# Stick-breaking attention of the later 512 tokens, computed between the expert rows by tanh, scan and product

## The chip, the cores and the metric

One core of one Trainium2 chip runs the whole program. The metric is the device time in microseconds (us) of one execution. The engines named below are PE (TensorE, matrix products and transposes), DVE (VectorE), ACT (ScalarE), POOL (GpSimd) and SP (SyncE, which here only issues DMAs).

## The reference, cut to what matters

One layer for 1024 tokens of 1024 features, float32: a mixer (gated linear attention beside stick-breaking attention, 8 heads of 64), an attention over 256 memory tokens, and PEER, in which each token gathers 128 expert rows (8 heads of 16) out of 16384.

```
z = q.k / 8 over all earlier tokens;  log_1m = log_sigmoid(-z) where s < t, else 0
A[t, s] = sigmoid(z_ts) * prod_{s<j<t} (1 - sigmoid(z_tj));  o_t = sum_s A[t, s] v_s        # 8 heads
h += [gla | o] @ w_out;  h += MemCrossAttn(rmsnorm(h))
h += sum over 128 experts e(t) of gate * gelu(u[e] . rmsnorm(h)) * v[e]                      # row of u|v: 8 KB
out = rmsnorm(h)
```

## The kernel before, in words

The tokens are split in halves of 512 (four blocks of 128 each). The mixer's projections are made for all 1024 tokens. `stick_phase` (from line 1569) then computes stick-breaking attention of both halves. Its unit of work is a tile: 128 keys on the partitions, up to 512 queries of one half on the columns, two heads at a time. `work` lists 48 pairs of tiles: per pair of heads four key blocks for the first half, eight for the second. Per tile PE makes z, ACT takes Abs, Exp, Ln (lines 1657 to 1659), DVE adds the positive part (line 1685), PE turns that into sums over later keys with a triangular product and a product with a running `carry` (lines 1721, 1725), ACT exponentiates (line 1650) and PE multiplies with the values (line 1751). GpSimd masks the diagonal tiles (line 1621). Six buffers lie between the engines.

After it come, for the first half alone, the output projection (`mixer_out_phase`), which also loads the residual x of all tokens into `co.H` (four loads of 1 MB), memory attention, and the first half's expert scores. Then `expert_phase` (from line 2207) runs through 1024 steps R, one for each of 128 experts of each of 8 token blocks:

- GpSimd gathers 128 rows of 8 KB (line 2014) into one of seven ring slots. It may reuse a slot once PE has read it (`row_used`).
- DVE takes the dot product of the row's first half with the token (line 2524), and runs one piece of the selection of the experts two groups ahead (`choice.select`, 16 pieces for each 16 rows).
- ACT takes Gelu (line 2626), multiplies by the gate (line 2628), scales the row's second half (line 2635), and once in 16 rows takes an Exp for the gate (line 1914).
- PE adds the row to an accumulator by eight transposes (line 2754).

Beside the rows, each engine has a function `later(R)` that runs the second half's remaining work at steps written in the table `Later`: the output projection (MIX, 64 matmul units, one a step), a norm, the memory query, the attention over memory (UNIT = 10 steps for each of 8 units), its output, a norm, and the second half's scores (KEYS), which must be there when the second half's rows begin at R = 512. The weights of these products come by SP through four slots `w_raw`. The order on each engine is the program's order, so an instruction that waits holds back all that its engine does later.

Shared state: `scratch`, `hb`, `own_acc`, `qt`, `w_raw` are buffers of the expert phase; `side[0..3]` are four PSUM banks for the work beside the rows.

Of the kernel before, what the change touches and what calls it, by code (L numbers as in the profile page):

```python
# [8 lines left out]
F32 = mybir.dt.float32  # L9
# [1559 lines left out]
def stick_phase(co, feat, tok, spare, mix_t, mix_b, negtri, negone):  # L1569
# [10 lines left out]
    NH = SEQ // HALF  # L1580
    QB = HALF // P
    S = 6
    PAIRS = SB_HEADS // 2

    rounds = [(-1, 0, 1), (0, 1, 7), (0, 1, 6), (-1, 0, 0), (0, 1, 5), (0, 1, 4), (0, 0, 3), (0, 1, 3), (0, 0, 2),
              (0, 1, 2), (0, 1, 1), (0, 1, 0)]
    work = [(pr + d, th, j, max(0, j - QB * th) * P) for pr in range(PAIRS + 1) for d, th, j in rounds
            if 0 <= pr + d < PAIRS and (pr < PAIRS or d)]  # L1590
    begun = [min(i for i, w in enumerate(work) if w[0] == pr) for pr in range(PAIRS)]
    M = len(work)
    N = 2 * M
    tile = lambda m: work[m // 2]
    diag = [tile(m)[2] >= QB * tile(m)[1] for m in range(N)]
    same = lambda n, m: n % 2 == m % 2 and tile(n)[1] == tile(m)[1]
    before = [max([n for n in range(m) if same(n, m)], default=None) for m in range(N)]
    ended = [w[:2] for w in work if w[2] == 0]

    adds = [0 if tile(m)[2] == 0 else (1 if not diag[m] else (2 if tile(m)[3] + P < HALF else 1)) for m in range(N)]  # L1600

    def upto(flags, n):

        return sum(flags[:n + 1])

    with ExitStack() as cx:
# [3 lines left out]
        carry = co.sb("stick_carry", [P, 2, NH, 2, HALF], ctx=cx)  # L1610
        pz = [cx.enter_context(nc.psum_tensor(f"stick_pz{j}", [P, HALF], F32)) for j in range(S)]
        po = [cx.enter_context(nc.psum_tensor(f"stick_po{j}", [P, HALF], F32)) for j in range(NH)]
        block = cx.enter_context(nc.Block())

        @block.gpsimd
        def _(pool):
            co.clear_stale(pool)

            def strict(ap, c0, done):

                pool.affine_select(out=ap[:, c0:c0 + P], in_=ap[:, c0:c0 + P], compare_op=ALU.is_gt, fill=0.0,  # L1621
                                   base=0, pattern=[[1, P]], channel_multiplier=-1).then_inc(done, 1)

            for i in range(M + 2):
                for n in (2 * i - 4, 2 * i - 3):
                    if n >= 0 and diag[n]:
                        pool.wait_ge(a_ready, n + 1)
                        strict(aw[:, n % S, :], tile(n)[3], a_masked)
                for m in (2 * i, 2 * i + 1):
                    if i < M and diag[m]:  # L1630
                        pool.wait_ge(sp_ready, m + 1)
                        strict(sps[:, m % S, :], tile(m)[3], sp_masked)

        @block.scalar
        def _(act):
# [3 lines left out]
            def queries(pr):  # L1639
                nc.scalar.activation(feat[:, pr, :], feat[:, pr, :], ACT.Copy, scale=SB_DH ** -0.5).then_inc(q_ready, 1)  # L1640

            queries(0)
            for i in range(M + 2):
                for n in (2 * i - 4, 2 * i - 3):
                    if n >= 0:
                        c0, s = tile(n)[3], n % S
# [4 lines left out]
                for m in (2 * i, 2 * i + 1):  # L1651
                    if m < N:
                        c0, s = tile(m)[3], m % S
# [6 lines left out]
                if i in (2, 3, 4):  # L1660
                    queries(i - 1)

        @block.vector
        def _(dve):

            for i in range(M + 5):
                n = 2 * (i - 4) + 1
                if 0 <= n < N and tile(n)[2] == 0:
                    pr, th, _, _ = tile(n)
                    dve.wait_ge(pv_done, n + 1)  # L1670
                    if th:
                        nc.vector.tensor_copy(mix_b[:, GLA_HEADS + pr, :], po[th][:, :]).then_inc(o_free, 1)
                    else:
                        hi, lo = (x[:, GLA_HEADS + pr, 0:HALF] for x in mix_t)
                        nc.vector.tensor_copy(hi, po[th][:, :]).then_inc(hi_ready, 1)
                        dve.wait_ge(hi_ready, pr + 1)
                        low(nc, lo, po[th][:, :], hi).then_inc(o_free, 1)
                two = (2 * i, 2 * i + 1) if i < M else ()
                for m in two:
                    c0, s = tile(m)[3], m % S  # L1680
                    if m >= S:
                        dve.wait_ge(carry_ready, upto(adds, m - S))
# [4 lines left out]
                for m in two:  # L1687
                    _, th, j, c0 = tile(m)
                    h, s = m % 2, m % S
                    if j > 0:  # L1690

                        k = QB * th + QB - 1 - j
                        new, old = carry[:, h, th, k % 2, :], carry[:, h, th, (k + 1) % 2, :]
                        if before[m] is not None:
                            dve.wait_ge(r_full, before[m] + 1)
                        c1 = c0 + P if diag[m] else c0
                        if diag[m]:
                            dve.wait_ge(sp_masked, upto(diag, m))
                        else:
                            dve.wait_ge(sp_ready, m + 1)  # L1700
                        if c1 < HALF:
                            dve.wait_ge(carry_ready, upto(adds, before[m]))
                            nc.vector.tensor_tensor(new[:, c1:], old[:, c1:], sps[:, s, c1:], ALU.add).then_inc(carry_ready, 1)
                        if diag[m]:
                            nc.vector.tensor_copy(new[:, c0:c1], sps[:, s, c0:c1]).then_inc(carry_ready, 1)

        @block.tensor
        def _(pe):
            for i in range(M + 3):
                if 0 <= i - 2 < M:  # L1710
                    _, th, j, c0 = work[i - 2]
                    for h in range(2):
                        n = 2 * (i - 2) + h
                        s = n % S
                        if diag[n]:
                            pe.wait_ge(sp_masked, upto(diag, n))
                        else:
                            pe.wait_ge(sp_ready, n + 1)
                        k = QB * th + QB - 1 - j
                        c1 = c0 + P if diag[n] else c0  # L1720
                        last = nc.tensor.matmul(pz[s][:, c0:], negtri[:, :], sps[:, s, c0:], start=False,  # L1721
                                                stop=(c1 == HALF), skip_group_check=True)
                        if c1 < HALF:
                            pe.wait_ge(carry_ready, upto(adds, before[n]))
                            last = nc.tensor.matmul(pz[s][:, c1:], negone[:, :], carry[:, h, th, (k + 1) % 2, c1:],
                                                    start=False, stop=True, skip_group_check=True)
                        last.then_inc(r_full, 1)
                if i < M:
                    pr, th, j, c0 = work[i]
# [4 lines left out]
                    for h in range(2):  # L1734
                        rows = slice(h * SB_DH, (h + 1) * SB_DH)
                        nc.tensor.matmul(pz[(2 * i + h) % S][:, c0:], feat[rows, F_KS - F_QS + pr, j * P:(j + 1) * P],
                                         feat[rows, pr, th * HALF + c0:(th + 1) * HALF], start=True, stop=False,
                                         skip_group_check=True).then_inc(z_full, 1)
                if 0 <= i - 3 < M:
                    pr, th, j, c0 = work[i - 3]  # L1740
                    n = 2 * (i - 3)
                    first = j == QB * th + QB - 1
                    if first and pr:
                        pe.wait_ge(o_free, ended.index((pr - 1, th)) + 1)
                    if diag[n]:
                        pe.wait_ge(a_masked, upto(diag, n + 1))
                    else:
                        pe.wait_ge(a_ready, n + 2)
                    for h in range(2):
                        rows = slice(h * SB_DH, (h + 1) * SB_DH)  # L1750
                        nc.tensor.matmul(po[th][rows, c0:], v[:, j, pr * P + h * SB_DH:pr * P + (h + 1) * SB_DH],
# [406 lines left out]
class Later:  # L2158
# [5 lines left out]
    NORM = 35  # L2164
    MIX = 2
    QNORM = MIX + 2 * KT * 4 + 3
    QUERY = QNORM + NORM
    ATTEND = QUERY + 2 * KT * 4 + 4
    UNIT = 10
    OUT = ATTEND + NB * UNIT + 12  # L2170
    FNORM = OUT + 2 * KT * 4 + 3
# [4 lines left out]
    def __init__(self):  # L2176
        begin = [self.MIX + 4 * p for p in range(2 * KT)] + [self.QUERY + 4 * p for p in range(2 * KT)]
        begin += [self.OUT + 4 * p for p in range(2 * KT)] + [self.KEYS + 4 * p for p in range(4 * PH)]
        self.fetch = {begin[i - self.SLOTS] + 4: i for i in range(self.SLOTS, self.N)}
        self.unit = {begin[i] + j: (i, j) for i in range(self.N) for j in range(4)}  # L2180
        self.add = {at + 32 * c + 31 + b: (2 * e + c, b) for e, at in enumerate((self.MIX, self.OUT))
                    for c in range(2) for b in range(4)}
        self.kept = {self.QUERY + 8 * m + 10: m for m in range(KT)}
        units = [(self.ATTEND + self.UNIT * u, u) for u in range(NB)]
        self.scores = {at + 2 * j: (u, j) for at, u in units for j in range(2)}
        self.maxima = {at + 5: u for at, u in units}
        self.exps = {at + 6: u for at, u in units}
        self.probs = {at + 8: u for at, u in units}
        self.turn = {at + 10: u for at, u in units}
        self.turned = {at + 12: u for at, u in units}  # L2190
        self.values = {at + 15 + 2 * j: (u, j) for at, u in units for j in range(2)}
        self.attended = {at + 20: u for at, u in units}
        norms = [(e, at) for e, at in enumerate((self.QNORM, self.FNORM))]
        self.square = {at + 1 + b: (e, b) for e, at in norms for b in range(4)}
        self.var = {at + 8: e for e, at in norms}
        self.guess = {at + 9: e for e, at in norms}
        self.refine = {at + 12 + j: (e, j) for e, at in norms for j in range(4)}
        self.scale = {at + 17 + 4 * b: (e, b) for e, at in norms for b in range(4)}
        self.across = {at + 19 + 4 * b: (e, b) for e, at in norms for b in range(4)}
        self.gain = {at + 22 + 4 * b: (e, b) for e, at in norms for b in range(4)}  # L2200
# [6 lines left out]
def expert_phase(co, choice, ring, scores, rstd, uv, gf, g_final, out, k_t, v_m, z_b, mix_b, w_out, w_mq, w_mo, w_pq,  # L2207
                 sub_keys, q_gain, gain):
# [21 lines left out]
    def pe_rows(R):  # L2230
# [19 lines left out]
        sem(n) for n in ("m_scored", "m_max", "m_probs", "m_normed", "m_turned", "m_turned_sb", "m_full", "o_kept"))  # L2250
    q_b = o_b = mix_b
    with ExitStack() as cx:
# [25 lines left out]
        m_stat = sb("m_stat", [P, 2, 4, 2])  # L2278
        m_ps = [side_ps[:, j, :].rearrange("p (h m) -> p h m", h=2) for j in range(2)]
        m_pt = [side_ps[:, 2 + j, :].rearrange("p (f t) -> p f t", t=P) for j in range(2)]  # L2280
        m_po = [side_ps[:, j, :].rearrange("p (f t) -> p f t", t=P) for j in range(2)]
        block = cx.enter_context(nc.Block())

# [29 lines left out]
        def _(sp):  # L2313
# [16 lines left out]

            for i in range(at.SLOTS):
                fetch(i)
# [617 lines left out]
```

## Time and profile before

| | us |
|---|---|
| median of 3 runs | 3633.78 (3633.17 to 3634.96) |
| the profiled execution | 3628.59, its span 3626.4 |
| PE, DVE, ACT, POOL busy | 2664.3, 2289.4, 2346.3, 1256.3 |

The profile is of one execution. Busy times of PE overlap with each other and are modelled at their ends. The stick phase begins after 384 us and ends at 593 us of the span; the expert phase begins at 967 us and ends with the span.

### The profile page before, as it was taken

How to read it: one execution, taken by the hardware profiler on the slowest of the kernel's cores; microseconds unless marked ns; L12 is line 12 of the kernel's file. 1: busy time of each engine (PE TensorE's matmuls, PEld its weight loads, DVE VectorE, ACT ScalarE, POOL GpSimd, SP SyncE). 2: the span in 40 equal slices, each digit the busy share in tenths (PEclk: the TensorE clock that was granted, in tenths of full speed). 3: DMA queues.
4: the chain of work that ended last, by engine and by line, in shares of the span. 5: the costliest groups of instructions: out<-in, count | busy, mean ns of one | idle time of the engine just before them, and what ended most of it. 6: DMA issues, size and time to landing. Idle time of an engine off the chain costs nothing.

```text
span 3626.4 us, 41556 instructions
## 1 busy us (share of the span) xinstructions
PE 2664.3 (73%) x13816; PEld 2003.4 (55%) x13816; DVE 2289.4 (63%) x5474; ACT 2346.3 (65%) x4227; POOL 1256.3 (35%) x1176
## 2 busy tenths in 40 slices
PE   7999998888877676667767777666666666666666
PEld 6777444777745544654455544555555554555554
DVE  4554444544566776777677666766676676667665
ACT  3221785423377777887687767777777777777775
POOL 0000110000234443444344334444444454444443
PEclk9999999999998899889979999767666667666666
DMA  2001002321599999999999999999999999999998
GB/s 111 18 19 47 1 1 102 119 82 58 220 420 420 419 420 415 406 415 420 420 414 420 419 418 410 410 416 418 417 412 416 417 410 416 417 416 410 419 415 339
DMA packets 177654, 1156.70 MB, mean 319 GB/s; under 512 B 19984, under 2 KB 22048, under 8 KB 46240
## 3 DMA queue, kind: packets, MB, share of 16 engines
q0 software_dynamic: 147456, 1073.81, 71.7%
q1 hardware_dynamic: 29984, 80.26, 6.1%
q8 instruction: 107, 1.75, 0.2%
q14 instruction: 107, 0.88, 0.1%
HBM read 1149.80 MB, written 4.19 MB: 318 GB/s over the span
## 4 chain that ended last, share of the span: by engine, by line
DMA 40%; ACT 14%; PE 8%; DVE 6%; issue 5%; POOL 1%; POOLq 0%; DVEq 0%; ACTq 0%
DMA early_rows<-in_uv,choice_index 24%; DMA rows<-in_uv,choice_index 16%; PE expert_acc L2754 7%; ACT early_rows L2635 4%; DVE early_rows L2524 3%; ACT rows L2635 2%; ACT L2626 2%; ACT L1914 2%; DVE rows L2524 2%; ACT expert_wt L2628 2%; ACT expert_wt L2626 1%; ACT choice_best L1914 1%; POOL rows L2014 0%; POOL early_rows L2014 0%; PE expert_acc L2741 0%
## 5 line engine op out<-in xcount | busy, mean ns | idle before, releaser
L2754 PE MATMUL expert_acc<-ident,early_rows 128*128 128x128 f32 x4648 | 826.6, 338 | 492.7 <-ACT early_rows L2635 492.0
L2754 PEld LDWEIGHTS expert_acc<-ident,early_rows 128*128 128x128 f32 x4648 | 680.7, 175 | 731.9 <-ACT early_rows L2635 704.2
L2524 DVE CUSTOM_DVE_ANT_0 early_rows<-early_rows,expert_xn 128x1024 f32<-128x1024 f32 x586 | 718.9, 1227 | 461.0 <-DMA early_rows<-in_uv,choice_index 459.3
L2014 POOL DMA_INDIRECT early_rows<-in_uv,choice_index x586 | 692.0, 1181 | 888.8 <-PE expert_acc L2754 742.4
L2754 PE MATMUL expert_acc<-ident,rows 128*128 128x128 f32 x3480 | 622.1, 340 | 369.4 <-ACT rows L2635 369.2
L2754 PEld LDWEIGHTS expert_acc<-ident,rows 128*128 128x128 f32 x3480 | 513.8, 177 | 545.3 <-ACT rows L2635 522.5
L2524 DVE CUSTOM_DVE_ANT_0 rows<-rows,expert_xn 128x1024 f32<-128x1024 f32 x438 | 537.1, 1226 | 339.6 <-DMA rows<-in_uv,choice_index 337.9
L2014 POOL DMA_INDIRECT rows<-in_uv,choice_index x438 | 514.6, 1175 | 644.2 <-PE expert_acc L2754 554.4
L2635 ACT ACTIVATE early_rows<-early_rows,expert_wt 128x1024 f32<-128x1024 f32 x581 | 667.3, 1149 | 18.9
L2626 ACT ACTIVATE expert_wt<-expert_dot 128x1 f32<-128x1 f32 x1024 | 204.9, 200 | 624.7 <-DVE expert_dot L2524 623.1
L2635 ACT ACTIVATE rows<-rows,expert_wt 128x1024 f32<-128x1024 f32 x435 | 499.6, 1149 | 14.2
L2628 ACT ACTIVATE expert_wt<-expert_wt,choice_gate 128x1 f32<-128x1 f32 x1024 | 301.5, 294 | 33.2
L2673 PE MATMUL expert_side<-z_b,expert_w_raw 128*128 128x512 f32 x256 | 135.3, 612 | 0.0
L2658 PE MATMUL expert_side<-expert_w_raw,mix_b 128*128 128x512 f32 x256 | 134.4, 607 | 0.0
L1685 DVE SCALAR_TENSOR_TENSOR heads<-stick_pz,stick_t 128x512 f32<-128x512 f32 (+3 forms) x96 | 53.5, 557 | 102.4 <-ACT stick_t L1659 102.2
L1621 POOL TENSOR_SCALAR_AFFINE_SELECT heads<-heads 128x128 f32<-128x128 f32 x64 | 20.7, 323 | 258.4 <-DVE heads L1685 258.2
L2626 ACT ACT_TABLE_LOAD x80 | 102.6, 1283 | 4.0 <-DVE expert_dot L2524 2.6
L2046 POOL IOTA choice_iota<- 128x16 f32 x1 | 0.1, 145 | 270.9 <-issue 270.9
L1721 PE MATMUL stick_pz<-heads,negtri 128*128 128x512 f32 (+3 forms) x192 | 83.5, 523 | 1.8 <-POOL heads L1621 1.2
L2524 DVE DVE_READ_ACCUMULATOR2_ANT expert_dot<- 128x1 f32 x1024 | 83.9, 82 | 0.0
L1914 ACT ACT_TABLE_LOAD x62 | 79.5, 1283 | 1.1
L1361 ACT ACTIVATE heads<-gla_po 128x256 f32<-128x256 f32 x16 | 5.3, 381 | 95.1 <-PE gla_po L1415 95.1
(369 smaller groups left out, 3956.2 us busy)
## 6 DMA issues: line engine op xcount, KB each, us to landing
early_rows<-in_uv,choice_index POOLq DMA_INDIRECT x586, 12.4
H<-in_x SPq DMA_DIRECT2D x8, 1024.0 KB, 10.6
pq_w_raw<-in_w_pq SPq DMA_DIRECT2D x16, 512.0 KB, 3.5
expert_w_raw<-in_w_pq SPq DMA_DIRECT2D x32, 256.0 KB, 9.0
rows<-in_uv,choice_index POOLq DMA_INDIRECT x438, 12.3
stick_w_raw<-in_w_feat SPq DMA_DIRECT2D x8, 512.0 KB, 3.5
tok_w_raw<-in_w_tok SPq DMA_DIRECT2D x8, 512.0 KB, 3.7
out_w_raw<-in_w_out SPq DMA_DIRECT2D x8, 512.0 KB, 4.2
```

The lines of the kernel that those rows point to most:

```text
L1621: pool.affine_select(out=ap[:, c0:c0 + P], in_=ap[:, c0:c0 + P], compare_op=ALU.is_gt, fill=0.0, base=0, pattern=[[1, P]], channel_multipl ...
L1685: nc.vector.scalar_tensor_tensor(sps[:, s, c0:], pz[s][:, c0:], 0.0, t[:, s, c0:], ALU.max, ALU.add).then_inc(sp_ready, 1)
L1721: last = nc.tensor.matmul(pz[s][:, c0:], negtri[:, :], sps[:, s, c0:], start=False, stop=(c1 == HALF), skip_group_check=True)
L1914: self.nc.scalar.activation(self.best[:, q, :], self.best[:, q, :], ACT.Exp, bias=self.small[:, 0, q:q + 1], accum_out=self.small[:, 1, q: ...
L2014: pool.indirect_dma_start(out=self.rows[R % self.ROWS], out_offset=None, in_=uv, in_offset=bass.IndirectOffsetOnAxis(ap=index, axis=0), bo ...
L2524: nc.vector.tensor_tensor_reduce(rows[R % ROWS][:, 0:D], rows[R % ROWS][:, 0:D], xn[:, :], 1.0, 0.0, ALU.mult, ALU.add, dot[:, h % 2, r:r ...
L2626: link(nc.scalar.activation(wt[:, s, 0, r:r + 1], dot[:, s, r:r + 1], ACT.Gelu))
L2628: weight = nc.scalar.activation(wt[:, s, 1, r:r + 1], wt[:, s, 0, r:r + 1], ACT.Copy, scale=gate[:, q, r:r + 1])
L2635: nc.scalar.activation(v, v, ACT.Copy, scale=wt[:, s, 1, r:r + 1]).then_inc(row_scaled, 1)
L2658: last = nc.tensor.matmul(side[j], mix_b[:, k, j * P:(j + 1) * P], w_raw[:, slot, :], start=k == 0, stop=k == KT - 1)
L2673: last = nc.tensor.matmul(side[n % 2], w_raw[:, slot, j * P:(j + 1) * P], x, start=k == 0, stop=k == KT - 1)
L2754: last_mm = nc.tensor.matmul(acc[:, k * P:(k + 1) * P], rows[R % ROWS][:, D + k * P:D + (k + 1) * P], co.ident[:, :], start=(r == 0 and k ...
```

## The change

`stick_phase` keeps the first half alone: 16 pairs of tiles, all on the diagonal, two pairs of heads interleaved (`LANES = 2`). On SP it gets DMAs that park data in HBM: the values v (2 MB), the second half's queries (1 MB), and `w`, the difference of each token's value and the value before it (2 MB), for which v is read back shifted by one token. DVE makes the four differences. `vcol` holds v at the block borders, by four loads of single elements.

The second half's attention is done in `expert_phase` in 32 turns (head by query block), one every 5 rows from R = 2. With 1 - sigmoid(z) = (1 - tanh(z/2))/2, a scan from the last key to the first gives the running product, and the product of that with w gives the output less the query's own value. Per turn: PE makes z with the queries on the partitions (640 to 1024 keys), ACT takes Tanh one step later, GpSimd halves it (`m * -0.5 + 0.5`) between two gathers, DVE scans it, PE transposes it, ACT copies it, PE multiplies with w, DVE adds `vcol`. `mix_b` gets the result. The x of the second half (2 loads of 1 MB) is loaded after the last turn instead of in `mixer_out_phase`. The table `Later` starts its old work at R = 168 instead of 2, in a closer order: three units in two steps, 26 steps for a norm instead of 35, UNIT = 7, and KEYS at R = 417 instead of 366.

```diff
-    rounds = [(-1, 0, 1), (0, 1, 7), ...]
-    work = [(pr + d, th, j, max(0, j - QB * th) * P) for pr in range(PAIRS + 1) for d, th, j in rounds
-            if 0 <= pr + d < PAIRS and (pr < PAIRS or d)]
+    work = [(pr + lane, j, j * P) for pr in range(0, PAIRS, LANES) for j in range(QB - 1, -1, -1) for lane in range(LANES)]
...
+        @block.sync
+        def _(sp):
+            sp.dma_start(park_v[1:SEQ + 1, :].rearrange("(b p) c -> p b c", p=P), v).then_inc(v_parked, 16)
+            sp.wait_ge(zeroed, 1)
+            sp.dma_start(park_v[0:1, :], zero[:, :]).then_inc(v_parked, 16)
+            sp.dma_start(park_q.rearrange("r p t -> p r t"), feat[:, 0:PAIRS, HALF:SEQ]).then_inc(q_parked, 16)
+            sp.wait_ge(v_parked, 32)
+            sp.dma_start(v_last[:, :, :], park_v[0:SEQ, :].rearrange("(b p) c -> p b c", p=P)).then_inc(shifted, 16)
+            for b in range(QB):
+                sp.dma_start(vcol[:, b, :], ...).then_inc(columns, 16)
+            sp.wait_ge(w_ready, NB // 2)
+            for pr in range(PAIRS):
+                sp.dma_start(park_w[pr]..., v_last[:, :, pr * P:(pr + 1) * P]).then_inc(w_parked, 16)
+            sp.wait_ge(q_parked, 16)
+            sp.wait_ge(columns, 16 * QB)
+            sp.wait_ge(w_parked, 16 * PAIRS)
...
+                if i in DIFF:
+                    b = 2 * DIFF[i]
+                    dve.wait_ge(shifted, 16)
+                    nc.vector.tensor_tensor(v_last[:, b:b + 2, :], v_last[:, b:b + 2, :], v[:, b:b + 2, :],
+                                            ALU.subtract).then_inc(w_ready, 1)
...
+    STICK, TURNS, STEP = 2, 4 * SB_HEADS, 5
+    MIX = STICK + STEP * (TURNS - 1) + 11
+        turns = [(self.STICK + self.STEP * u, u) for u in range(self.TURNS)]
+        self.z, self.tanh, self.halve, self.scan, self.flip, self.flipped, self.weigh, self.stick = (
+            {at + after: u for at, u in turns} for after in (0, 1, 2, 3, 6, 7, 8, 10))
...
                     ring.gather(pool, R, index[:, q, r:r + 1], uv)
+                    if R - ROWS + 1 in at.halve:
+                        u = at.halve[R - ROWS + 1]
+                        pool.wait_ge(tanh_ready, u + 1)
+                        pool.tensor_scalar(m, m, -0.5, 0.5, ALU.mult, ALU.add).then_inc(halved, 1)
...
+                if R in at.scan:                                                  # DVE
+                    dve.wait_ge(halved, u + 1)
+                    nc.vector.tensor_tensor_scan(m, m, m, 1.0, ALU.mult, ALU.min).then_inc(scanned, 1)
+                if R in at.stick:
+                    dve.wait_ge(o_full, u + 1)
+                    nc.vector.tensor_scalar(mix_b[...], side[2][feats, 0:P], vcol[...], None, ALU.add).then_inc(o_taken, 1)
...
+                if R in at.tanh:                                                  # ACT
+                    act.wait_ge(z_full, u + 1)
+                    nc.scalar.activation(probs[u % 2][:, 0:ended], z_ps[:, 0:ended], ACT.Tanh,
+                                         scale=0.5 * SB_DH ** -0.5).then_inc(tanh_ready, 1)
+                if R in at.flipped:
+                    act.wait_ge(p_turned, u + 1)
+                    nc.scalar.activation(probs_t[:, 0:ended], flip_ps[:, 0:ended], ACT.Copy).then_inc(p_kept, 1)
...
+                if R in at.z:                                                     # PE
+                    nc.tensor.matmul(z_ps[:, 0:HALF], q, co.H[feats, HB + pr, 0:HALF], start=True, stop=True)
+                    nc.tensor.matmul(z_ps[:, HALF:ended], q, co.H[feats, HB + pr, HALF:ended], ...)
+                    nc.tensor.matmul(z_ps[:, ended - P:ended], co.ident[:, :], above[:, :], ...).then_inc(z_full, 1)
+                if R in at.flip:
+                    pe.wait_ge(scanned, u + 1)
+                    for j in range(ended // P):
+                        last = nc.tensor.transpose(flip_ps[:, cols], probs[u % 2][:, cols], co.ident[:, :])
+                if R in at.weigh:
+                    for j in range(ended // P):
+                        last = nc.tensor.matmul(side[2][feats, 0:P], pair_w[pr][:, j, feats], probs_t[:, j * P:(j + 1) * P], ...)
```

## Rows read from the trace of the kernel before

**Rows 1.** Stages: stretch, length, busy PE PEld DVE ACT POOL, PEclk, DMA share, GB/s.
```profile
384.00:593.00 209.00, 202.75 (x736) 85.92 (x736) 101.39 (x228) 182.36 (x390) 39.64 (x128) 0.98 0.00 1
...
967.00:3627.00 2660.00, 1786.23 (x9248) 1359.81 (x9248) 1833.62 (x4634) 1949.40 (x3518) 1201.97 (x1020) 0.79 1.00 413
...
1000.00:1178.00 178.00, 129.65 (x645) 83.19 (x644) 119.38 (x302) 129.42 (x234) 73.32 (x67) 0.90 1.01 420
...
1413.00:1650.00 237.00, 152.79 (x968) 134.96 (x968) 178.44 (x453) 200.39 (x365) 108.98 (x93) 0.83 1.00 410
```

**Rows 2.** Groups by form, stick phase, ACT: busy us, mean ns, idle before.
```profile
L1657 ACT ACTIVATE stick_t<-stick_pz 128x512 f32<-128x512 f32 x48 | 28.3, 589 | 3.0 <-PE stick_pz L1736 3.0
L1658 ACT ACTIVATE stick_t<-stick_t 128x512 f32<-128x512 f32 x48 | 30.2, 630 | 1.5
L1650 ACT ACTIVATE tok<-stick_pz 128x512 f32<-128x512 f32 x48 | 26.8, 588 | 9.0 <-PE stick_pz L1725 9.0
L1658 ACT ACTIVATE stick_t<-stick_t 128x128 f32<-128x128 f32 x16 | 5.0, 310 | 0.5
```

**Rows 3.** Instructions in order of time, the stick phase's ends: start us, us.
```profile
383.84 1.28 ACT L1637 ACT_TABLE_LOAD   x1 [0.47 <-ACTq L1534]
...
387.07 0.28 ACT L1657 ACTIVATE stick_t<-stick_pz 128x128 f32<-128x128 f32 x1 [0.88 <-PE stick_pz L1736]
...
589.07 0.60 ACT L1650 ACTIVATE tok<-stick_pz 128x512 f32<-128x512 f32 x1 [0.91 <-PE stick_pz L1725]
...
592.93 1.28 ACT L823 ACT_TABLE_LOAD   x1 [3.26 <-PEq L1606]
```

**Rows 4.** The chain that ended last, one row's way through the engines: start us, us.
```profile
1018.91 1.23 DVE rows L2524
1020.17 0.21 ACT expert_wt L2626
1020.41 0.30 ACT expert_wt L2628
1020.74 1.16 ACT rows L2635
1021.94 1.11 PE expert_acc L2754 x8
1023.10 0.73 issue
```

**Rows 5.** Instructions in order of time: a gather's issue, and DVE with rows already landed.
```profile
1023.82 0.99 POOL L2014 DMA_INDIRECT rows<-in_uv,choice_index  x1 [1.52 <-PE expert_acc L2754]
...
971.66 1.20 DVE L2524 CUSTOM_DVE_ANT_0 early_rows<-early_rows,expert_xn 128x1024 f32<-128x1024 f32 x1
...
973.32 1.21 DVE L2524 CUSTOM_DVE_ANT_0 early_rows<-early_rows,expert_xn 128x1024 f32<-128x1024 f32 x1
```

**Rows 6.** Lines L1174 (ns min/median/max) and, by form, POOL: nearest to scan and halving.
```profile
L1174 DVE TENSOR_TENSOR_SCAN decay<-decay_keep,decay_gate x2: 2291/2291/2291, 115.7 to 126.7; 128x1024 f32<-128x1024 f32 x2
...
L1253 POOL COPY gla_vb<-heads 128x512 f32<-128x512 f32 x2 | 1.6, 802 | 0.0
L1086 POOL MEMSET decay_keep<- 128x1024 f32 x1 | 1.0, 953 | 72.5 <-issue 72.5
```

**Rows 7.** DMAs: size, us from issue to landing (of L2014: min/median/max).
```profile
DMA to landing us min/median/max: 5.8/12.4/15.1
...
H<-in_x SPq DMA_DIRECT2D x8, 1024.0 KB, 10.6
out<-expert_hb SPq DMA_DIRECT2D x8, 512.0 KB, 9.8
```

**Rows 8.** The page's groups: table loads ahead of Gelu and Exp; the products beside the rows.
```profile
L2673 PE MATMUL expert_side<-z_b,expert_w_raw 128*128 128x512 f32 x256 | 135.3, 612 | 0.0
...
L2626 ACT ACT_TABLE_LOAD x80 | 102.6, 1283 | 4.0 <-DVE expert_dot L2524 2.6
...
L1914 ACT ACT_TABLE_LOAD x62 | 79.5, 1283 | 1.1
```

More of the change, by code:

```diff
@@ L1579, in stick_phase @@
     q_ready, act_done, hi_ready = sem("q_ready"), sem("act_done"), sem("hi_ready")
-    NH = SEQ // HALF
+    zeroed, v_parked, q_parked, shifted, columns, w_ready, w_parked = (
+        sem(n) for n in ("zeroed", "v_parked", "q_parked", "shifted", "columns", "w_ready", "w_parked"))
+    park_v, park_q, park_w = park
     QB = HALF // P
@@ L1594, in stick_phase, with upto @@
     tile = lambda m: work[m // 2]
-    diag = [tile(m)[2] >= QB * tile(m)[1] for m in range(N)]
-    same = lambda n, m: n % 2 == m % 2 and tile(n)[1] == tile(m)[1]
+    same = lambda n, m: n % 2 == m % 2 and tile(n)[0] % LANES == tile(m)[0] % LANES
     before = [max([n for n in range(m) if same(n, m)], default=None) for m in range(N)]
[L1598 to L1604, printed above, removed]
+    adds = [0 if tile(m)[1] == 0 else (2 if tile(m)[2] + P < HALF else 1) for m in range(N)]
+    DIFF = {6 + 2 * d: d for d in range(NB // 2)}
+    def upto(n):
+        return sum(adds[:n + 1])
     with ExitStack() as cx:
@@ L1639, in queries @@
             def queries(pr):
[L1640 removed]
+                nc.scalar.activation(feat[:, pr, 0:HALF], feat[:, pr, 0:HALF], ACT.Copy, scale=SB_DH ** -0.5).then_inc(q_ready, 1)
             queries(0)
+            queries(1)
             for i in range(M + 2):
@@ L2176, in __init__ @@
     def __init__(self):
[L2177 to L2182, printed above, removed]
@@ L2192, in __init__ @@
-        self.attended = {at + 20: u for at, u in units}
+        third = [2 * x // 3 for x in range(8 * KT)]
+        rows = [self.MIX + x for x in third] + [self.QUERY + x for x in third] + [self.OUT + x for x in third]
+        rows += [self.KEYS + x for x in range(16 * PH)]
+        self.fetch = {rows[4 * (i - self.SLOTS) + 3] + 1: i for i in range(self.SLOTS, self.N)}
+        self.unit, self.add = {}, {}
+        for x, R in enumerate(rows):
+            self.unit.setdefault(R, []).append((x // 4, x % 4))
@@ new lines, in __init__ @@
+        units = [(self.ATTEND + self.UNIT * u, u) for u in range(NB)]
+        self.scores = {at + j: (u, j) for at, u in units for j in range(2)}
+        self.maxima = {at + 2: u for at, u in units}
+        self.exps = {at + 3: u for at, u in units}
+        self.probs = {at + 5: u for at, u in units}
+        self.turn = {at + 6: u for at, u in units}
+        self.turned = {at + 8: u for at, u in units}
+        self.values = {at + 9 + j: (u, j) for at, u in units for j in range(2)}
+        self.attended = {at + 12: u for at, u in units}
@@ L2346, in _ @@
             co.clear_stale(pool)
+            pool.memset(above[:, :], -1.0e30).then_inc(mask_ready, 1)
+            pool.wait_ge(mask_ready, 1)
+            pool.affine_select(out=above[:, :], in_=above[:, :], compare_op=ALU.is_ge, fill=0.0, base=0,
+                               pattern=[[1, P]], channel_multiplier=-1).then_inc(mask_ready, 1)
             def group(g, q):
@@ L2422, in later @@
             def later(R):
+                if R in at.scan:
+                    u = at.scan[R]
+                    _, _, _, ended = turn(u)
+                    dve.wait_ge(halved, u + 1)
+                    m = probs[u % 2][:, ended - 1::-1]
+                    nc.vector.tensor_tensor_scan(m, m, m, 1.0, ALU.mult, ALU.min).then_inc(scanned, 1)
+                if R in at.stick:
+                    u = at.stick[R]
+                    pr, feats, b, _ = turn(u)
+                    dve.wait_ge(o_full, u + 1)
+                    nc.vector.tensor_scalar(mix_b[feats, GLA_HEADS + pr, b * P:(b + 1) * P], side[2][feats, 0:P],
+                                            vcol[feats, b, pr:pr + 1], None, ALU.add).then_inc(o_taken, 1)
                 if R in at.maxima:
```

243 lines of the change are left out of this document (157 added, 86 removed).

## The prediction

> **What bounds the kernel now.** I read the stages first, by busy time in stretches, then the groups of the stick phase, then the chain that ended last, then the single operations that come nearest to the new ones.
>
> The stages [rows 1] show two different machines. In the stick phase (384 to 593 us) ACT is busy for 182.36 of 209 us while the DMA engines move 1 GB/s: ACT's four operations per tile set the pace, and the DMA engines are free. From 967 us to the end it is the reverse. The DMA share is 1.00 over 2660 us at 413 GB/s, with no compute engine above 73% (ACT). A gather is 128 rows of 8 KB, 1.049 MB, so at the 420 GB/s of the calm stretch it takes 2.50 us; 2660 us over 1024 steps are 2.60 us a step, the rest being weights and stores. A step that computes more costs nothing there as long as each engine, and each loop of waits through several engines, stays under some 2.5 us per step.
>
> The change takes ACT-bound time away where the DMA engines idle, and puts the work, and 5 MB of traffic, where the DMA engines are full. Three things decide: what the short stick phase costs, what the traffic costs, and whether a turn of five steps still fits in 5 x 2.50 = 12.5 us.
>
> **Stick phase, what goes.** The old one runs from the table load at 383.84 to the next phase's at 592.93 us, 209.1 us [rows 3]. The new one has 32 tiles (16 pairs), eight of each width 512, 384, 256, 128. ACT needs for a 512-wide tile 0.589 + 2 x 0.630 + 0.588 = 2.44 us; the Abs, Exp and Ln of a 128-wide one are about 0.3 each by the 0.310 of its Exp, with the second Exp 1.2 in all [rows 2]. Cost grows evenly with width, so the mean over the four widths is (2.44 + 1.2) / 2 = 1.82 and 32 tiles take 58 us. The same count for before (48 wide tiles at 2.44, 16 of each other width at 2.0, 1.6 and 1.2) gives 194 us, against 589.67 - 387.07 = 202.6 us measured [rows 3], so 1.04 times the count: 61 us. Around it stay 3.2 us at the start and 3.3 us at the end [rows 3], and about 2 us of query scaling and of DVE's four differences. Sum 70 us, a gain of 139 us.
>
> The new DMAs lie beside it. Parking v (2 MB), reading it back shifted behind the parked queries (1 MB), and writing w (2 MB) are a chain through SP. A 1 MB load landed in 10.6 us and a store of 512 KB in 9.8 us, both partly in company of other traffic [rows 7]; by these v is parked and read back some 25 us into the phase, near the sixth pair, where DVE first waits for it. The last difference comes at pair 12 of 16, about 50 us in, and the 2 MB of w need another 5 (420 GB/s) to 39 us (four stores one after another at 9.8); I take 18, so the phase ends at 384 + 71. With the worst it ends 20 us later. The four loads of single elements lie between; no row shows such a load, and I bound them by 0 and by the store's 9.8 us each, hidden by the compute up to about 20 us together. Net stick gain: 138 us, 115 to 141.
>
> **Traffic in the expert phase.** Queries and w come back (1 + 2 MB) and x moves in (2 MB): 5.2 MB, at 413 GB/s 12.7 us if the DMA engines stay full [rows 1]. Where the turns themselves are slower than the DMA engines, the 3 MB read in the turns cost nothing, and 5 us remain for x. Taking x's 2 MB out of the mixer's output phase saves nothing: that phase starts with weights, and 1 MB of memory tokens still comes with it.
>
> **The turn as a loop.** This is where I expect the loss. GpSimd halves turn u only behind the gather of step h + 6 (h is the turn's third step), and that gather waits until PE has read row h - 1. DVE at step h + 1 waits for the halving, with all later dot products behind it, and row h + 4, which releases the next turn's halving, is one of them. So one lap is five steps long:
> - from the start of the dot product of row h - 1 through Gelu, gate, scaling, PE's eight transposes and 0.73 us of issue to the gather: 1023.82 - 1018.91 = 4.91 us [rows 4, 5];
> - the gather's issue 0.99 us [rows 5];
> - the halving of 640 to 1024 columns, 832 in the mean. No row has it. A fill of 1024 took 0.953 us, so 0.8 is the low end; a copy of 512 took 0.802, so 1.3 is a high end by width [rows 6]. I take 1.0, nearer to the fill, plus 0.35 for the two handovers;
> - the scan: 2.291 us for 1024 columns [rows 6], by width 1.9 us in the mean;
> - the rest of step h + 1 on DVE (selection, 0.35 us), two intervals of dot products with rows already landed, 1.66 us each [rows 5], and the addition of `vcol`, 0.25.
>
> Sum 4.91 + 0.99 + 1.35 + 1.9 + 0.35 + 3.32 + 0.25 = 13.1 us, above 12.5. Two things lengthen it at times: PE's z matmuls (a 128x512 product shows 612 ns [rows 8]) stand one row ahead of row h - 1, worth 0.3 us, and the Exp of the gate with its two table loads of 1283 ns [rows 8] falls into the dependent part of about 6 of 32 laps, 0.3 us in the mean. I take 13.7. Between gathers that land early or late (5.8 to 15.1 us [rows 7]) the ring evens out bursts, but not a lap that is always longer. 32 turns then take 438 us instead of 400: 38 us lost.
>
> By load alone the engines fit: ACT 5 x 1.89 (129.42 of 178 us at 2.60 a step [rows 1]) + two operations of some 0.9 us = 11.3 us; DVE 5 x 1.74 + 2.15 = 10.9; on PE a turn's three z products, its transposes and its products with w (about 3 us, an estimate by the 612 ns of a 512-column product [rows 8]) stand where five 512-column units stood before.
>
> The SBUF page of the Trainium skill (SBUF — State Buffer, Who interferes with whom) says that a VectorE instruction with two SBUF inputs and a GpSimd one that reads SBUF block each other for a whole instruction. In the loop DVE is idle when the halving runs, so by that rule too the lap stays 13.7; where DVE is not waiting, the rule would put up to 1.2 us of a dot product before the halving. No row before shows such a pair.
>
> **What is packed closer.** The old work now runs at 1.5 units per step, and the memory attention at 7 steps a unit. ACT was busy for 200.39 of 237 us there, 22.0 us per unit of 10 steps; less three steps of 1.89 it is 16.3 of 17.5 us [rows 1]. DVE asks for the maxima one step behind the score matmuls instead of three, and waits about 1 us per unit. It fits, barely; I take 6 us for both, 0 to 15. KEYS still ends 25 steps ahead of its use. The first turn's queries come with the first gathers: 2 us.
>
> **Sum.** Against the profiled execution, 3628.6: -138 (stick) + 38 (turns) + 5 (x) + 6 (closer packing) + 2 (start) = -87, 3541.6 us. The runs' median is 5.2 us above that execution, so 3547 us.
>
> **Rivals.**
> 1. All hidden, 3511 us. The lap stays under 12.5 us because narrow blocks (640 columns: scan 1.4, halving 0.8) make up for wide ones. Then only traffic counts: 3633.8 - 138 + 12.7 + 2. For it: the DMA share of 1.00 with all engines under 85% [rows 1]. Against: the lap's rows already add up to 13.1. Chance 0.25, 3500 to 3525.
> 2. A longer turn, 3600 us. Tanh may need its own table beside Gelu's: two loads of 1.283 us per turn bring ACT to 13.9 us plus the catching up; or halving and dot products exclude each other for 1 to 2 us. Either makes the lap about 15.4: 3547 + 32 x 1.7 = 3601. No run before shows tanh.
> 3. The stick phase's DMAs end last: single elements and w take 20 to 30 us more than the compute, 3570 us. For it: the four w stores hang on the last difference. Chance 0.05.
> 4. The other side, slower. GpSimd has never done arithmetic between gathers here. If a switch between the two kinds costs it time, that time is in the lap in full. It decides from 13.7 + 87/32 = 16.4 us a lap, so at 2.7 us more per turn than I count; at 4 us more the time is 3547 + 128 = 3675. For it: gathers issue in 0.99 us but one that follows closely takes up to 2 us; against: a fill or copy needs under 1 us. Chance 0.07.
>
> The forecast has the rest, 0.43, with its own range of 3525 to 3575. The range over the cases runs from 3506, inside rival 1, to 3602, the centre of rival 2. A change under 0.2% (7 us) could not be told from none. Slower by more: rival 4 from its deciding point, 0.06; within: 0.02; faster: 0.92.
>
> **What would show it.** Stick phase: from its first table load to the next phase's about 71 us; if SP's stores end after ACT by over 5 us, rival 3. Turns: step time between R = 2 and 162 about 2.74 us with a DMA share clearly under 1.00 and 385 GB/s; DVE's scan waiting on POOL by 1.5 to 3 us each time shows the loop, a share of 1.00 shows rival 1. A table load in front of each Tanh shows rival 2. A halving over 2 us, or gathers behind it over 2 us, shows 4. After R = 545 nothing changes: 2.60 us a step. The prediction is wrong if the lap's longest part is another, such as ACT, or if the compressed norm or attention steps lose more than 15 us.

## The result and the profile after

The changed kernel takes 3603.38 us (3596.47 to 3604.11, 4 runs) against 3633.48 for the one before; ratio 0.9915, interval 0.9898 to 0.9932. It is faster by 30 us, 0.85% and clear of the noise, where 87 us were forecast. The profiled execution took 3596.47 us; before it was 3628.59, so the traces differ by 32.

The phases, from the trace after. Instructions in order of time (start, duration), ACT and SP; they answer to [rows 3]:

```profile
384.37 1.28 ACT L1659 ACT_TABLE_LOAD   x1 [0.47 <-ACTq L1534]
...
450.62 1.28 ACT L823 ACT_TABLE_LOAD   x1 [3.41 <-PEq L1606]
...
432.64 4.27 SPq L1630 DMA_DIRECT2D park_w<-stick_v_last  x4
...
484.37 43.71 SPq L318 DMA_DIRECT2D mk_w_raw<-in_w_mk  x8
```

The stick phase is 66.3 us long (209.1 before). Its last stores are issued before 437 us; such a store landed 5.4 us after its issue in the median, so they hide behind the compute, which ends at 447 us. Stages, with the columns of [rows 1]:

```profile
817.00:1328.00 511.00, 364.67 (x2110) 283.81 (x2111) 347.88 (x809) 348.96 (x614) 268.23 (x200) 0.86 0.91 345
...
1640.00:1830.00 190.00, 125.77 (x782) 110.03 (x781) 130.32 (x340) 155.11 (x284) 79.01 (x69) 0.84 0.96 385
...
2200.00:3590.00 1390.00, 917.29 (x4526) 734.85 (x4524) 945.12 (x2370) 999.04 (x1803) 652.37 (x535) 0.71 1.00 411
```

In the 32 turns (817 to 1328 us) the DMA engines move 345 GB/s instead of the 420 of the calm stretch before, and no compute engine is above 72% of its time. Some loop of waits sets the pace. Who waits, 820 to 1320 us (total, times, longest):

```profile
DVE expert_w_raw L2503 <- POOL expert_w_raw L2433: 137.4, 32, 9.8
...
ACT expert_w_raw L2658 <- PE expert_side L2798: 52.5, 25, 4.8
...
DVE mix_b L2508 <- PE expert_side L2817: 15.9, 12, 3.4
...
DVE rows L2611 <- DMA rows<-in_uv,choice_index: 4.5, 2, 3.4
```

Before, DVE's main wait was for rows to land. Now rows have landed and DVE waits at each of the 32 scans for GpSimd's halving, 4.3 us in the mean. The new operations themselves are short (ns min/median/max):

```profile
L2433 POOL TENSOR_SCALAR expert_w_raw<-expert_w_raw x32: 735/900/1061, 833.8 to 1315.9; 128x640 f32<-128x640 f32 x8, 128x768 f32<-128x768 f32 x8, 128x896 f32<-128x896 f32 x8, 128x1024 f32<-128x1024 f32 x8
...
L2503 DVE TENSOR_TENSOR_SCAN expert_w_raw<-expert_w_raw x32: 1491/1892/2293, 834.6 to 1317.0; 128x640 f32<-128x640 f32 x8, 128x768 f32<-128x768 f32 x8, 128x896 f32<-128x896 f32 x8, 128x1024 f32<-128x1024 f32 x8
```

One lap in order of time, from the dot product of row h - 1 at 1084.62 us. ACT has scaled that row at 1087.6 us, but PE first does z for the coming tanh (L2795 to L2798), then the row; only then come the gather, the halving and the scan:

```profile
1084.62 1.22 DVE L2611 CUSTOM_DVE_ANT_0 rows<-rows,expert_xn 128x1024 f32<-128x1024 f32 x1
...
1086.32 1.12 PE L2795 MATMUL expert_side<-H,expert_spare 64*128 64x512 f32 x2
...
1086.44 1.15 ACT L2739 ACTIVATE rows<-rows,expert_wt 128x1024 f32<-128x1024 f32 x1
...
1087.28 0.59 PE L2796 MATMUL expert_side<-H,expert_spare 64*128 64x256 f32 x2
...
1087.80 0.49 PE L2798 MATMUL expert_side<-expert_above,ident 128*128 128x128 f32 x2
1088.13 1.04 PE L2895 MATMUL expert_acc<-ident,rows 128*128 128x128 f32 x8
...
1089.96 0.99 POOL L2029 DMA_INDIRECT rows<-in_uv,choice_index  x1 [1.73 <-PE expert_acc L2895]
...
1090.98 0.84 POOL L2433 TENSOR_SCALAR expert_w_raw<-expert_w_raw 128x768 f32<-128x768 f32 x1
...
1091.86 1.76 DVE L2503 TENSOR_TENSOR_SCAN expert_w_raw<-expert_w_raw 128x768 f32<-128x768 f32 x1 [2.93 <-POOL expert_w_raw L2433]
```

Averaged over the turns, from the starts and ends of these instructions, a lap is 15.6 us, and 32 of them are the 499 us that steps 2 to 162 took: dot product to gather 7.0 (5.3 in the lap above), gather 1.0, halving with its handovers 1.0, scan 1.9, rest of the step 0.4, the two intervals of dot products 1.7 and 2.6.

### The profile page after: what moved, and what is told of

It reads as the page before. It is cut to its first block, busy times and chain, and to the rows that moved or that the text cites. A ratio compares the mean times of both kernels' runs of the same rounds, so it can differ in the third digit from the quotient of the medians.

```text
span 3594.8 us, 41774 instructions
## 1 busy us (share of the span) xinstructions
PE 2669.4 (74%) x14136; PEld 2061.8 (57%) x14136; DVE 2279.1 (63%) x5394; ACT 2259.8 (63%) x4033; POOL 1322.2 (37%) x1147
## 4 chain that ended last, share of the span: by engine, by line
DMA 30%; ACT 17%; PE 14%; DVE 8%; issue 6%; POOL 2%; POOLq 0%; DVEq 0%; ACTq 0%
DMA early_rows<-in_uv,choice_index 19%; DMA rows<-in_uv,choice_index 10%; PE expert_acc L2895 9%; ACT early_rows L2739 4%; DVE early_rows L2611 3%; ACT rows L2739 3%; ACT L2730 2%; ACT expert_wt L2732 2%; ACT L1929 2%; DVE rows L2611 2%; ACT expert_wt L2730 1%; PE expert_side L2764 1%; POOL early_rows L2029 1%; DVE expert_w_raw L2503 1%; PE expert_side L2795 1%
## 5 line engine op out<-in xcount | busy, mean ns | idle before, releaser
L2029 POOL DMA_INDIRECT early_rows<-in_uv,choice_index x586 | 725.9, 1239 | 939.4 <-PE expert_acc L2895 764.2
L2029 POOL DMA_INDIRECT rows<-in_uv,choice_index x438 | 536.7, 1225 | 595.6 <-PE expert_acc L2895 521.8
L2503 DVE TENSOR_TENSOR_SCAN expert_w_raw<-expert_w_raw 128x640 f32<-128x640 f32 (+3 forms) x32 | 60.5, 1891 | 137.4 <-POOL expert_w_raw L2433 137.4
L2658 ACT ACTIVATE expert_w_raw<-expert_side 128x640 f32<-128x640 f32 (+3 forms) x32 | 27.6, 862 | 53.7 <-PE expert_side L2798 52.5
L158 ACT ACTIVATE pq_w_hi<-pq_w_raw 128x1024 fp32r<-128x1024 f32 x16 | 16.9, 1056 | 69.4 <-PE keys_pq L171 67.8
```

The lines of the kernel that those rows point to most:

```text
L2029: pool.indirect_dma_start(out=self.rows[R % self.ROWS], out_offset=None, in_=uv, in_offset=bass.IndirectOffsetOnAxis(ap=index, axis=0), bo ...
L2503: nc.vector.tensor_tensor_scan(m, m, m, 1.0, ALU.mult, ALU.min).then_inc(scanned, 1)
L2658: nc.scalar.activation(probs[u % 2][:, 0:ended], z_ps[:, 0:ended], ACT.Tanh, scale=0.5 * SB_DH ** -0.5).then_inc(tanh_ready, 1)
```

## The experiments

Ratios are to the kernel before on the same chip, with 95% intervals. A ratio's worth in us is taken against 3628 us.

**Scan two steps later.**
```diff
-            {at + after: u for at, u in turns} for after in (0, 1, 2, 3, 6, 7, 8, 10))
+            {at + after: u for at, u in turns} for after in (0, 1, 2, 5, 8, 9, 10, 12))
```
The stages behind the turns start two steps later too.

> The changed kernel with the scan and all behind it two steps later in each turn (scan at step 5 of the turn instead of 3, transposes 8, copy 9, product 10, addition 12; the later stages start 2 steps later). Theory loop: a lap runs from the dot product of row h-1 over ACT, PE, the gather, the halving and the scan to the dot product of row h+4, 15.6 us in the trace of the changed kernel. With the scan two steps later two intervals of dot products (1.71 + 2.59 us) fall out of it, so it is 11.3 us and the DMA engines set the pace: steps 2 to 162 at about 2.6 us instead of 3.12, GB/s in that stretch from 345 to over 400, the time about 3603 - 80 = 3523 us (3505 to 3545). Rival load: the turns are slow because an engine or the DMA engines have more to do; then it stays at 3603 within 8. Rival GpSimd: a gather that follows arithmetic is slower by itself; then it also stays near 3603.

Measured 3588.1 us, ratio 0.9887 (0.9870 to 0.9904): 10 us won, not 80. The theory in this form fell. The waits show why (820 to 1300 us):

```profile
POOL early_rows L2029 <- PE expert_acc L2895: 99.9, 41, 7.6
DVE mix_b L2508 <- PE expert_side L2817: 99.5, 26, 10.1
```

The wait for the halving is gone (4.5 us are left of 129), and 99.5 us of waiting for PE's product with w stand in its place. Steps 2 to 162 took 484 us, 15.1 a turn. There is a second handover behind the first, over DVE, ACT and PE without GpSimd. But this edit also made it worse: a turn starts every 5 steps, so the product, now at step 10, falls into the same step as the z of the turn two later. In 30 of 32 turns PE does it right behind z; in the changed kernel in none. Two lines of this run in order of time, the end of a turn's z and the product of the turn two before:

```profile
1085.87 0.49 PE L2798 MATMUL expert_side<-expert_above,ident 128*128 128x128 f32 x2
1086.29 1.96 PE L2817 MATMUL expert_side<-expert_spare,expert_own_acc 128*64 128x128 f32 x16
```

How much of the 99.5 us comes from this meeting and how much from the handover was not separated.

**No halving at all.** GpSimd's instruction is left out, so the later half's attention is wrong; `dve.wait_ge(halved, u + 1)` becomes `dve.wait_ge(tanh_ready, u + 1)`.

> The changed kernel without GpSimd's halving; the scan waits for the tanh instead and scans it as it is, so the attention of the later half is wrong. Theory loop: GpSimd, the gather ahead of it and PE leave the lap, which is now dot product of h-1, ACT, tanh, scan, two dot products: about 1.3 + 1.7 + 1.0 + 0.9 + 1.9 + 0.4 + 4.3 = 11.5 us; DMA bound, about 3525 us (3505 to 3545), as with the later scan, although the same DVE, ACT and PE work is done. Rival load: only GpSimd's 32 x 0.9 us of work goes, and GpSimd is at 52% there, so no more than 10 us are won: 3593 or above. Rival GpSimd (arithmetic between gathers is dear): also about 3525, and so told apart by the run with the later scan alone.

Measured 3540.75 us, ratio 0.9759 (0.9743 to 0.9776): 57 us less for leaving out 29 us of work on an engine that was half idle. DVE still waited 63.7 us for the product with w, which may be why it did not reach 3525. Between these two runs it stayed open whether GpSimd's arithmetic is dear in itself.

**z one step earlier.**
```diff
-            ... for after in (0, 1, 2, 3, 6, 7, 8, 10))
+            ... for after in (-1, 1, 2, 3, 6, 7, 8, 10))
```

> The changed kernel with each turn's three z matmuls one step earlier (step -1 of the turn instead of 0), so that they no longer stand on PE right ahead of the transposes of row h-1. Theory loop: the 1.36 us between ACT's end and PE's start in the lap fall to about 0.3, the lap from 15.6 to 14.6 us: 32 x 1.0 = 32 us less, 3571 us (3560 to 3585). Rival load: PE's work is the same, so nothing changes: 3603 within 8. If PE were not in the lap at all, also 3603.

Measured 3598.96 us, ratio 0.9916 (0.9900 to 0.9933): nothing. The expectation missed. ACT's end to PE's start did fall from 1.3 to 0.6 us in the mean, but PE's end to the gather rose from 0.9 to 1.9: z now delays the row before, and with it the gather queued ahead of the one that counts. PE is in the lap for all it does in a few rows.

**The scan and the addition later.** Steps (0, 1, 2, 5, 8, 9, 10, 13).

> As the run with the later scan (scan at step 5 of a turn, transposes 8, copy 9, product with w 10), and DVE's addition of vcol at step 13 instead of 12, three steps behind the product on PE. In the run with the scan alone DVE's wait for the halving (129 us in the turns) was gone, and a wait of 99.5 us for the product with w stood in its place. Theory chains: every step that couples DVE to PE or GpSimd with two steps or less between them makes a lap of its own; with the addition three steps behind, part of the 99 us goes: 3588 - 20 = 3568 us (3545 to 3580). Rival load: what is left is work on PE at a low clock and on ACT; then 3588 within 8 and the wait shows up on another pair.

Measured 3571.59 us, ratio 0.9842 (0.9824 to 0.9861), 16 us better than with the scan alone; the wait for the product is down from 99.5 to 68.7 us. The product is still at step 10, behind a z.

**All couplings apart.**
```diff
-            ... for after in (0, 1, 2, 3, 6, 7, 8, 10))
+            ... for after in (0, 2, 3, 6, 9, 10, 11, 14))
-    MIX = STICK + STEP * (TURNS - 1) + 11
+    MIX = STICK + STEP * (TURNS - 1) + 15
```

> All couplings of a turn drawn apart: z at 0, tanh 2 (was 1), halving 3, scan 6 (three steps behind the halving instead of one), transposes 9, copy 10, product 11, addition 14. The same work on each engine as in the changed kernel. Theory chains: the waits are hidden, steps 2 to 162 take 2.60 to 2.70 us instead of 3.12, and the time is 3597 - 70 = 3527 us (3510 to 3550). Rival load (PE at half clock, ACT with its table loads, DVE): the work of a turn does not fit beside five rows whatever the order; then steps of 2.95 us and more and a time above 3570.

Measured 3527.75 us, ratio 0.9725 (0.9709 to 0.9742): 69 us better than the changed kernel with exactly its work. The stage, and two of the waits (820 to 1240 us): DVE waits for landing rows again.

```profile
817.00:1262.00 445.00, 339.79 (x2124) 268.95 (x2125) 372.80 (x822) 350.33 (x621) 267.97 (x202) 0.89 0.98 399
```
```profile
DVE early_rows L2611 <- DMA early_rows<-in_uv,choice_index: 25.9, 34, 2.3
DVE rows L2611 <- DMA rows<-in_uv,choice_index: 22.5, 24, 3.4
```

The rival by load is out: DVE is busy for 84% of this stretch and ACT for 79%, and it fits.

Against the run before this one only two things differ, apart from all steps behind z being one later: tanh stands two steps behind z instead of one, and the product no longer falls into the step of a z. Together they are worth 42 us, more than the later scan and addition (27). ACT's wait for z went with them, 52.2 us before and 3.5 here. Which of the two counts was not tested.

**The halving on DVE.** Steps as in the changed kernel; DVE does `tensor_scalar(m, m, -0.5, 0.5, mult, add)` before the scan.

> The halving done by DVE just before the scan instead of by GpSimd, steps as in the changed kernel. Theory chains: GpSimd, its gather and PE leave the lap, DVE gets 32 x 0.5 to 0.9 us more. The run without halving was at 3541, so about 3541 + 10 = 3551 us (3545 to 3575), 45 us better than with GpSimd's help. Rival: DVE is the bound, and taking work from it is what counts; then it is no better than the changed kernel, 3597 or more.

Measured 3546.66 us, ratio 0.9775 (0.9758 to 0.9791). DVE needs 486 to 692 ns for it, 19 us in all, and the kernel is 51 us faster than with GpSimd's help. All other distances are as in the changed kernel, so of the 69 us that the version with couplings apart gained, GpSimd's place in the lap was worth about 51. DVE still waits 47.1 us for the product, which shows the second handover without the meeting of product and z.

**The memory attention one step later.**
```diff
-        self.maxima = {at + 2: u for at, u in units}
+        self.maxima = {at + 3: u for at, u in units}
```
and all behind it likewise.

> The changed kernel with the memory attention's maxima, and all behind them, one step later in each unit (the maxima two steps behind the last score product instead of one); UNIT stays 7. In the changed kernel the stretch from 1640 to 1830 us moves 385 GB/s instead of about 418. Theory chains: DVE's wait for the scores is the cause; the stretch comes back to about 410 GB/s, 8 to 12 us less: 3587 us. Rival load: ACT's table loads fill the units (16.3 of 17.5 us by count); then no change, 3597 within 5.

Measured 3587.02 us, ratio 0.9883 (0.9867 to 0.9900), 12 us less than the changed kernel (the two intervals overlap slightly; the stretch shows it better). The stretch from 1640 us, against 385 GB/s above:

```profile
1640.00:1830.00 190.00, 126.99 (x815) 110.32 (x814) 140.35 (x359) 163.56 (x302) 86.34 (x72) 0.88 1.00 412
```

**x moved alone, in the kernel before.** `loads[2:4]` issued behind the first four weights of the expert phase; the add waits for them.

> The kernel before with one part of the change alone: the second half's x (2 MB) is loaded at the start of the expert phase instead of in the mixer's output phase. The changed kernel's mixer output phase was 6.6 us shorter than before (33.7 instead of 40.3 us from its first weight load to the next phase's). Theory: its two x loads less did that, so here too the phase is 6 to 7 us shorter and the expert phase is 5 us longer (2.1 MB at 418 GB/s): 3632 us, within 5 of before. Rival: something else shortened it, such as the memory tokens' place; then the phase stays at 40 us and the time is 3638.

Measured 3630.35 us, ratio 1.0003 (0.9993 to 1.0012). SP's issues show the mixer's output phase at 33.6 us (592.72 to 626.27) instead of 40.3 and DVE's dot products show the expert phase's steps 2 to 42 at 2.79 us instead of 2.65. What the one phase gains, the other gives back: the kernel's time is unchanged. The issues:

```profile
592.72 0.80 SPq L318 DMA_DIRECT2D out_w_raw<-in_w_out  x2
...
626.27 43.69 SPq L318 DMA_DIRECT2D mk_w_raw<-in_w_mk  x8
```

**Both edits together, and who halves then.**

> The turns with all couplings drawn apart (first of the two edits, 70 us) and the memory attention's maxima one step later (second, 10 us), together. Theory chains: the two waits lie in different stretches, so their gains add: 3597 - 80 = 3517 us (3508 to 3525), with the DMA engines at 400 GB/s or more from 820 us on. Rival: what one frees the other stretch gives back, 3527.

> As the run with both edits, and the halving on DVE. Theory chains: once the couplings are apart, it does not matter which engine halves as long as it has time; DVE is at 84% of its time there and gets 0.5 to 0.9 us a turn more, GpSimd is at 60%: 3517 to 3527 us, equal or a little slower than with GpSimd. Rival: GpSimd's arithmetic itself costs gathers; then this one is faster by 10 us or more.

> The changed kernel once more, beside the two above on one chip: 3597 us within 6 (ratio to before 0.9915).

Measured: 3518.31 us, ratio 0.9700 (0.9687 to 0.9713) with GpSimd halving; 3517.84, 0.9696 (0.9683 to 0.9709) with DVE halving; 3598.74, 0.9922 (0.9907 to 0.9937) for the changed kernel again. The gains add, 80 us in all, and the result is 3.0% under the kernel before. Apart, it does not matter who halves, within the 5 us that the intervals allow. That closes what the runs with the later scan and without halving left open: GpSimd's arithmetic adds nothing to the kernel's time. It does not relieve DVE either. In the stage DVE is busy for 379.74 us with GpSimd halving and for 376.70 with its own halving in them; the last section shows why. The stage with GpSimd halving:

```profile
817.00:1262.00 445.00, 346.77 (x2149) 274.89 (x2150) 379.74 (x827) 354.72 (x630) 271.17 (x205) 0.89 0.99 404
```

## Why the prediction was wrong

- **Stick phase**: held. Forecast -138 us, measured 209.1 - 66.3 = 142.8, 2 us outside the 115 to 141 that I gave this term. DVE's differences and the DMAs hid entirely.
- **x out of the mixer's output phase "saves nothing"**: wrong. It saved 6.7 us there, shown alone by the run with x moved. Probably the loads hold up the weights that the phase waits for: a piece of `w_out` landed 4.2 us after its issue in the median with them and 3.6 without. That this is the way was not tested.
- **Traffic**: held. In the run with x moved, x alone cost about 5.5 us (40 steps by 0.14).
- **The turn as a loop**: right as a mechanism, and the step that failed by its size. Forecast 13.7 us a lap, 438 us for the 32 turns; measured 15.6 and 499 (3.12 a step). These 61 us are more than the whole miss of 55; the stick phase and x took some 11 back. The version with couplings apart takes 425 us (2.65 a step) for the same work, so 74 us are the price of the waits and of what follows from them. Of the terms, the scan (1.9) and the gather (1.0) held, and the halving took less (1.0 with handovers, 1.35 counted). The term 4.91 for dot product to gather, 5.5 with the 0.3 each that I added for z and for the table loads, was 7.0. It had been read off one row in a calm stretch. In the turns the row starts on PE 1.3 us after ACT has scaled it, with z before it, instead of 0.3; the transposes take 1.4 us in the mean instead of 1.1; from dot product to scaled row it is 3.4 us instead of 3.0, of which the table loads (0.3) had been counted. The last interval of dot products was 2.6 instead of 1.7, partly DVE's wait for the product with w.
- **What I didn't see**: the handovers behind the first. I counted the addition of `vcol` at 0.25 us of work and not as a wait on PE two steps behind, and tanh, one step behind z, not at all. With the halving off GpSimd and all distances kept the time is 3547; only with these two handovers drawn apart as well (the halving back on GpSimd, three steps ahead of the scan) is it 3528. The 3588 of the run with the later scan is not their price alone, since product and z meet in it.
- **Closer packing**, 6 us (0 to 15): about 15 in the attention units by the shortfall of the stretch (190 us by 385 instead of the 417 GB/s of the stretches beside it, an estimate), 9 to 12 of it given back by one step of distance.
- **Rivals**: a tanh table load did not come: the page after has one load fewer at each of its two lines than before [rows 8], and none at the tanh (L2658). The gather behind a halving took 2.0 us in the mean, and over 2 us in 19 of 32 turns, where gathers before took 1.1. It goes with DVE's scan and not with GpSimd's arithmetic: without any halving, the gathers that overlap a scan still took 1.9 us in the mean and the others 1.3. This gather is not in the lap, and the price per turn that rival 4 needed did not come, so it is out. Exclusion between halving and dot products, the rule of the Trainium skill's page SBUF — State Buffer (Who interferes with whom), can't be seen in the changed kernel, where DVE stood idle at every halving; the runs with couplings apart agree with it (a dot product of 2.57 us instead of 1.2 with a halving in it, last section). Rival 2's time (3601) came out by another cause, and that the measured time lies beside it says nothing for that rival.

```profile
L2730 ACT ACT_TABLE_LOAD x79 | 101.4, 1283 | 4.0 <-DVE expert_dot L2611 2.6
...
L1929 ACT ACT_TABLE_LOAD x61 | 78.3, 1283 | 1.1
```

The sum by what was measured, in the traces: -142.8 (stick) - 6.7 (the rest ahead of the first dot product, x) + 117.8 (from the first dot product to the end, 2775.8 us instead of 2658.0) = -31.7. Of the 117.8, by estimate, 12.5 are traffic (5.24 MB), 89 the turns (511 us by 345 instead of 418 GB/s) and 15 the attention units. The 74 us above are less than 89, since the version with couplings apart still moves 399 GB/s there. The reader who compares with the forecast of 38 us for the turns should take the 61 us above, which are counted as the forecast was.

## What to carry to other kernels

When side work is laid between the steps of a pipeline over several engines, count the steps between producer and consumer in each handover, and not only the work: here the same work at greater distances was 69 us faster. An engine that waits in order for one far down the pipeline closes a lap, and the lap's length over its steps is the pace. Draw all handovers apart at once, since taking one lap out may only show the next, and look at which pieces fall into the same step of one engine afterwards. Size a lap from rows of the crowded state, with every instruction that stands before the released one on each engine, not from one calm passage.

## What the runs showed of the hardware

**The clock.** PE's granted clock fell within the turns. In the run with the later scan, PE sat idle for 4.47 us behind ACT's two table loads, and then eight transposes took 1.97 us instead of 1.09, z with its mask 4.35 instead of 2.2 (128 columns wider). The two stretches, columns as before:

```profile
1084.00:1095.00 11.00, 8.85 (x64) 6.89 (x62) 7.12 (x15) 7.61 (x13) 5.43 (x5) 1.00 0.98 379
1099.00:1108.00 9.00, 8.69 (x26) 5.69 (x27) 0.35 (x2) 4.25 (x8) 0.99 (x1) 0.50 0.91 366
```

The clock is 1.00 of full speed (2.4 GHz) in the one and 0.50 (1.2 GHz) in the other. The changed kernel has the same, eight transposes in 1.97 us behind 3.65 us of idle time at 1101.43 us. So a wait in a tight lap is paid again by slower matmuls behind it. How much of the 74 us this makes was not measured by itself.

**GpSimd and DVE hold each other up.** With both edits and GpSimd halving, the two engines work at the same time. A dot product, which takes at most 1.3 us in the changed kernel, takes up to 2.6 when a halving falls into it; a halving, at most 1.06 us in the changed kernel, takes up to 1.8. Instructions in order of time, a dot product that a halving falls into and its row on GpSimd:

```profile
1111.46 2.57 DVE L2611 CUSTOM_DVE_ANT_0 early_rows<-early_rows,expert_xn 128x1024 f32<-128x1024 f32 x1
...
1112.11 0.84 POOL L2433 TENSOR_SCALAR expert_w_raw<-expert_w_raw 128x768 f32<-128x768 f32 x1
```

Over the turns this lengthens the dot products by 13 us, and short instructions of the selection too; with DVE halving, no dot product is longer than 1.3 us. That is why moving the halving to GpSimd gave DVE no time back: the 19 us of work came back as waits inside its own instructions.
